# Encoder trunk, two layers on one core: the B-C products moved into a projection unit, and a re-divided entry

## The chip, the cores and the metric

The kernel runs on one NeuronCore of a Trainium2 chip. The metric is the device time of one execution in microseconds. A core has five engines with queues of their own: TensorE (PE; its weight loads are listed apart as PEld), VectorE (DVE), ScalarE (ACT), GpSimd (POOL) and SyncE (SP), which here only issues transfers. They meet at semaphores alone.

## The reference: what is computed

Two sequences of 256 tokens (512 tokens, width 1024) are layer-normalised and go through two layers:

```
proj = h @ w_in                       # q, k, v, z, x/B/C, dt
attn_out = window_attention(rope(q), rope(k), v, sink)
xbc = silu(depthwise_conv(xbc, w, b));  xs, bm, cm = split(xbc)
y = bidir_ssd(xs, dt_raw, dt_bias, a_log, bm, cm) + d * xs
ssd_out = rms_norm(y * silu(z), g)
h = layer_norm(alpha * h + concat(attn_out, ssd_out) @ w_out)
gate, val = split(h @ w_up);  gate = depthwise_conv(gate, w3, b3)
h = layer_norm(alpha * h + (silu(gate) * val) @ w_down)
```

In `bidir_ssd` each 128-token block needs the product of its C rows with the B rows (`einsum("bcqgn,bcsgn->bcgqs", cc, bc)`), in two groups. These are the B-C products of this change.

## The kernel before

**Units.** Every weight matrix is cut into units of 128x1024 (512 KB): 27 per layer for the input projection (unit 0 is dt, 1 k, 2 v, 3 to 6 q, 7 to 10 the B and C channels, 11 to 18 x, 19 to 26 z), 12 for the output projection, 44 up, 22 down. Five `raw`, `whi` and `wlo` slots form a ring. SP loads a unit into `raw`; `split` on ACT writes its high part `whi`. The low part `wlo` = raw - whi comes from DVE, or, for the units in `BY_DMA`, in two steps: ACT writes -whi, and a transfer issued by POOL adds the weights to it. A product is three fp32r matmuls (`by_columns`, `three`: high by high, high by low, low by high), 24 of 512 columns per unit of the projection.

**The order of the mixer.** `mixer_schedule()` writes one list, `SCHED`; each engine walks the whole list and does what concerns it. Step n has ("G", n), the unit's 24 matmuls, and around it the work of earlier units. The names that matter:

- AS, AM, AX, AD, AN, PT, AV (attention, eight items i = n - 8): scores on PE (L1255); mask, maximum and negation on DVE (L1622 to L1627); exponentials on ACT (L808); denominator and reciprocal on DVE (L1635); scaling of `sc` on POOL (L580); 32x32 transpose into `p_t` on DVE (L1648); values on PE in the middle of units 12, 14, 16 and 17 (`AV_AT`, L896), their low part `alo` on DVE (L1638).
- E, F, F1, F2, F3, SILU, SIL2 (the convolution): centre tap on ACT (L720), four taps on DVE (L1476), tanh on ACT (L755), the last product on DVE (L1483, into `bc` or `xsc`), counted by `silu_done`.
- T: transposes of an x channel block on PE (L1181), which wait for `silu_done` of its block. XS: product of `xsc` by a column on POOL (L588).
- CB: the B-C products, two fp32 matmuls of 256 columns for each block i = 0 to 3 (L1189), copied to `cb` by ACT (L781).
- MV: four `heads` tiles on POOL (L599). SB, SF: decay matmuls on PE (L1215, L1226). SC: their caps on DVE (L1579).

Small products (CB, T, VT, DTT, SD, AA, AO and the values' first claim) share banks 6 and 7 by turns: `wait_aux_free` lets a use begin when the one two before it has been read. The use two before CB(0) is the first value product, free once `alo` has been written (`al_done`). PE's queue is in order, so a product that waits holds the whole next unit.

**Entry.** PE runs 18 small matmuls (`keep_warm`, L905), then transposes the first two normalised token tiles (L1081), then 8 more, then `entry_units` begins units 0 to 2 (L917) on the first sequence. DVE takes moments and normalises all four token tiles; ACT makes the high part of unit 1 (`split(1)`) and then the activations' high part (`highs`, L648, L657); POOL makes the low part of the first sequence's activations (`lows(0)`, L550).

## Time and profile before

| | |
|---|---|
| median of 3 runs | 1298.28 us (1296.52 to 1298.59) |
| profiled execution | 1298.11 us |
| its span, first to last instruction | 1296.3 us (1.8 us lie around it) |
| mean granted TensorE clock | 0.998 |
| PE, PEld | 1280.9 us (99%), 1059.5 us (82%) |
| DVE, ACT, POOL | 801.7 us (62%), 609.2 us (47%), 131.0 us (10%) |
| chain that ended last | PE 92%, DVE 6%, ACT 1%, issue 1% |

Busy time is the time in which an instruction of the engine was under way. PE's matmuls overlap (one of 512 columns is listed with 390 ns, the next starts 0.23 us after it), so 99% busy hides short waits; those are read from start times. The shares of DVE, ACT and POOL are means over stages with very different loads.

### The profile page before, as it was taken

To read this page: it belongs to the slowest core of one execution; us is meant where nothing else is said; L and a number is where in the kernel's file an instruction comes from. 1 tells how busy PE (TensorE), PEld (TensorE's weight loads), DVE (VectorE), ACT (ScalarE), POOL (GpSimd) and SP (SyncE) were. 2 spreads that over 40 slices of the span, in tenths; PEclk is the share of its full clock that TensorE was granted. 3 is DMA by queue.
4 is the path that set the end of the run, shared out by engine and by line. 5 is a ranking of instruction groups with operands and counts; after the bars stand their busy time and mean duration, and the time that the engine had idled before them with its cause. 6 is when DMAs were issued, how large, how long until landed. Compare 5 with 4: busy or idle time off the path is not lost.

```text
span 1296.3 us, 17993 instructions
## 1 busy us (share of the span) xinstructions
PE 1280.9 (99%) x7456; PEld 1059.5 (82%) x7456; DVE 801.7 (62%) x1071; ACT 609.2 (47%) x913; POOL 131.0 (10%) x125
## 2 busy tenths in 40 slices
PE   9999999999999999999999999999999999999997
PEld 8877778889888888888898777788888888888886
DVE  7888898866444444342378998979654444443425
ACT  5766766436333333311276776653553333332112
POOL 2034511001000000000020354000100000000000
PEclk9999999999999999999999999999999999999999
DMA  5465565423333333323134656563133323223222
GB/s 200 158 147 115 132 146 138 172 77 103 98 98 98 98 98 98 130 98 97 54 127 150 151 114 150 129 179 130 66 114 98 98 98 96 96 93 129 96 95 111
DMA packets 43872, 151.36 MB, mean 117 GB/s; under 512 B 4912, under 2 KB 9424, under 8 KB 42640
## 3 DMA queue, kind: packets, MB, share of 16 engines
q1 hardware_dynamic: 38160, 130.01, 30.2%
q0 software_dynamic: 5632, 20.21, 9.1%
q8 instruction: 59, 0.97, 0.3%
q14 instruction: 21, 0.17, 0.0%
HBM read 141.81 MB, written 6.29 MB: 114 GB/s over the span
## 4 chain that ended last, share of the span: by engine, by line
PE 92%; DVE 6%; ACT 1%; issue 1%; DMA 0%; POOL 0%; SPq 0%; DVEq 0%
PE ps L870 17%; PE ps L871 17%; PE ps L872 17%; PE ps L1028 9%; PE ps L1029 9%; PE ps L1030 9%; PE ps L917 5%; PE ps L1242 2%; DVE cv L1476 2%; PE ps L896 1%; PE ps L1020 1%; DVE ast L1624 1%; PE ps L1189 1%; PE ps L1255 1%; PE ps L1226 1%
## 5 line engine op out<-in xcount | busy, mean ns | idle before, releaser
L870 PE MATMUL ps<-hhi,whi 128*128 128x512 f32 x1040 | 411.2, 395 | 0.9 <-DVE cv L1476 0.7
L871 PE MATMUL ps<-hlo,whi 128*128 128x512 f32 x1040 | 405.5, 390 | 0.0
L872 PE MATMUL ps<-hhi,wlo 128*128 128x512 f32 x1040 | 405.2, 390 | 0.0
L619 ACT ACTIVATE whi<-raw 128x1024 fp32r<-128x1024 f32 x208 | 219.4, 1057 | 214.6 <-DMA raw<-in_units 214.6
L1313 DVE TENSOR_TENSOR wlo<-raw,whi 128x1024 fp32r<-128x1024 f32 x170 | 207.8, 1224 | 149.4 <-ACT whi L619 149.4
L870 PEld LDWEIGHTS ps<-hhi,whi 128*128 128x128 f32 x1040 | 195.4, 188 | 49.3 <-issue 6.7
L872 PEld LDWEIGHTS ps<-hhi,wlo 128*128 128x128 f32 x1040 | 195.5, 188 | 41.3
L871 PEld LDWEIGHTS ps<-hlo,whi 128*128 128x128 f32 x1040 | 195.6, 188 | 39.4
L1028 PE MATMUL ps<-whi,uhi 128*128 128x512 f32 x352 | 137.1, 390 | 0.0
L1030 PE MATMUL ps<-wlo,uhi 128*128 128x512 f32 x352 | 137.0, 389 | 0.0
L1029 PE MATMUL ps<-whi,ulo 128*128 128x512 f32 x352 | 136.9, 389 | 0.0
L1689 DVE SCALAR_TENSOR_TENSOR gcv<-ps,pf,gcv 128x510 f32<-128x510 f32 x44 | 32.9, 749 | 157.3 <-ACT gcv L840 157.3
L840 ACT ACTIVATE gcv<-ps,pf 128x512 f32<-128x512 f32 x44 | 34.3, 780 | 169.0 <-PE ps L872 162.2
L1699 DVE TENSOR_TENSOR guf<-gsg,ps 128x512 f32<-128x512 f32 x44 | 30.2, 687 | 79.0 <-PE ps L872 78.4
L1476 DVE SCALAR_TENSOR_TENSOR cv<-ps,pm,cv 128x508 f32<-128x508 f32 (+1 forms) x96 | 71.4, 744 | 11.2 <-ACT cv L720 4.9
L1028 PEld LDWEIGHTS ps<-whi,uhi 128*128 128x128 f32 x352 | 66.1, 188 | 13.7
L1030 PEld LDWEIGHTS ps<-wlo,uhi 128*128 128x128 f32 x352 | 66.1, 188 | 13.7
L1029 PEld LDWEIGHTS ps<-whi,ulo 128*128 128x128 f32 x352 | 66.1, 188 | 13.6
L1028 PE MATMUL ps<-whi,ahi 128*128 128x512 f32 x192 | 75.8, 395 | 0.2
L1029 PE MATMUL ps<-whi,alo 128*128 128x512 f32 x192 | 74.8, 389 | 0.0
L1030 PE MATMUL ps<-wlo,ahi 128*128 128x512 f32 x192 | 74.7, 389 | 0.0
L550 POOL TENSOR_TENSOR hlo<-hfm,hhi 128x512 fp32r<-128x512 f32 x16 | 21.9, 1375 | 513.0 <-ACT hhi L657 512.7
(182 smaller groups left out, 1548.7 us busy)
## 6 DMA issues: line engine op xcount, KB each, us to landing
raw<-in_units SPq DMA_DIRECT2D x208, 512.0 KB, 3.5
wlo<-in_units POOLq DMA_DIRECT2D x38, 512.0 KB, 5.5
gb<-in_gb SPq DMA_DIRECT2D x5, 1024.0 KB, 5.5
h_kept<-hb SPq DMA_DIRECT2D x2, 2048.0 KB, 8.9
ha<-h_kept SPq DMA_DIRECT2D x2, 2048.0 KB, 9.6
hb<-in_x SPq DMA_DIRECT2D x4, 512.0 KB, 5.8
v_rep<-v_tm SPq DMA_DIRECT2D x32, 64.0 KB, 2.1
out_y<-hb SPq DMA_DIRECT2D x8, 256.0 KB, 2.0
```

Of the source, the lines that this page charges most:

```text
L619: A(whi[:, m % RING, :], raw[:, m % RING, :], ACT.Copy).then_inc(unit_hi, 1)
L840: A(gcv[:], ps[:, bank, :], ACT.Identity, scale=pf[:, k * 3 + w0 + 1:k * 3 + w0 + 2], bias=pf[:, k + v0:k + v0 + 1]).then_inc(glu_center, 1)
L870: mm(out, whi[:, slot, cols], xhi, start=start, stop=False)
L871: mm(out, whi[:, slot, cols], xlo, start=False, stop=False)
L872: return mm(out, wlo[:, slot, cols], xhi, start=False, stop=stop)
L917: last = mm(out, w, x, start=c == 0 and kind == "hi hi", stop=stop, skip_group_check=True)
L1028: mm(ps[:, bank, :], xhi[:, rows], whi[:, slot, cols], start=start, stop=False)
L1029: mm(ps[:, bank, :], xlo[:, rows], whi[:, slot, cols], start=False, stop=False)
L1030: return mm(ps[:, bank, :], xhi[:, rows], wlo[:, slot, cols], start=False, stop=stop)
L1313: V.tensor_tensor(wlo[:, m % RING, :], raw[:, m % RING, :], f(whi[:, m % RING, :]), ALU.subtract).then_inc(unit_split, 1)
L1476: V.scalar_tensor_tensor(out=dst[:, :, lo:hi], in0=src[:, :, lo + s:hi + s], scalar=pmc("conv_w", 5 * j + tap, 5 * j + tap + 1), in1=dst[: ...
L1689: V.scalar_tensor_tensor(out=dst[:, :, 1:SEQ], in0=src[:, :, 0:SEQ - 1], scalar=pf[:, k * 3 + w0:k * 3 + w0 + 1], in1=dst[:, :, 1:SEQ], op ...
```

## The change

It has four parts. (a) The B-C products of blocks 0 and 2 are issued by PE in the middle of units 13 and 15 (`CB_AT`, `mixed`), where they stood ahead of units 13 and 15; ACT copies them after its exponentials and not before. (b) Unit 11 joins `BY_DMA`: DVE's subtraction for it goes, ACT writes one more negated copy, POOL issues one more transfer. (c) On DVE the transpose PT goes ahead of the product SIL2 of the same step, and at n = 17 the caps SC(0) go ahead of SIL2; on POOL the `heads` tiles are made one step earlier. (d) At the entry ACT normalises the first token tile in two halves (`entry_act`), after DVE has written its shift (`entry_shift`); POOL makes the high part of unit 1 (`entry_high`); the second warm-up has 4 matmuls, not 8.

```diff
-BY_DMA = range(12, 31)
+BY_DMA = range(11, 31)
+CB_AT = {13: 0, 15: 2}
@@ mixer_schedule
-        if n in (13, 15):
+        if n in CB_AT:
             steps += [("CB", n - 12)]
-        if n in (12, 14):
-            steps += [("CB", n - 12)]
+        if n + 1 in CB_AT:
+            steps += [("CB", CB_AT[n + 1])]
         steps += [("SH" if n >= U_CONV else "S", n + AHEAD)]
...
         if 1 <= i < 8:
-            steps += [("SIL2", n - 1 - U_CONV)]
+            steps += [("PT", i - 1), ("SIL2", n - 1 - U_CONV)]
...
-            steps += [("PT", i - 1)]
+        if n == 15:
+            steps += [("MV", 0), ("MV", 1)]
...
             steps += [("SILU", n - U_CONV)]
+            if n == 17:
+                steps += [("SB", 0), ("SC", 0)]
...
-            if n == 17:
+            if n == 16:
                 steps += [("MV", 2), ("MV", 3)]
@@ POOL
+            def entry_high():
+                pool.wait_ge(raw_loaded[1], 16)
+                nc.gpsimd.tensor_copy(whi[:, 1, :], raw[:, 1, :]).then_inc(entry_hi, 1)
...
                 if L == 0:
+                    entry_high()
                     lows(0)
@@ ACT
+            act.wait_ge(entry_shift, 1)
+            for half in range(2):
+                x = hb[:, 0, half * 512:(half + 1) * 512]
+                A(x, x, ACT.Identity, scale=st[:, 0, 3:4], bias=st[:, 0, 0:1]).then_inc(entry_act, 1)
             split(0)
-            split(1)
             highs(0, 0)
@@ PE
+            def mixed(L, i):
+                pe.wait_ge(silu_done, L * N_CONV + 4)
+                wait_aux_free(pe, L, ("CB", i))
+                for g in range(2):
+                    last = mm(...)
+                last.then_inc(aux_full, 1)
...
-            keep_warm(8, 7)
+            keep_warm(4, 7)
...
-                        between = functools.partial(values, L, AV_AT[i]) if i in AV_AT else None
+                        between = None
+                        if i in AV_AT:
+                            between = functools.partial(values, L, AV_AT[i])
+                        elif i in CB_AT:
+                            between = functools.partial(mixed, L, CB_AT[i])
@@ DVE
-            normed_first(0)
+            rstd(0, 0)
+            dve.wait_ge(ln_rstd, 1)
+            V.tensor_scalar(st[:, 0, 0:1], st[:, 0, 1:2], st[:, 0, 3:4], -1.0, ALU.mult, ALU.mult).then_inc(entry_shift, 1)
             normed_first(1)
```

PE's queue between unit 12 and unit 13 of layer 0, before. `ps<-qk` are the scores AS(4), `ps<-bc` the B-C products of block 0, then comes unit 13; in brackets the semaphores that a row waits for.

```order
L872 MATMUL ps<-hhi,wlo 128x512
L1255 MATMUL ps<-qk 128x256 [waits as_exp]
L1255 MATMUL ps<-qk 128x256 x3
L1189 MATMUL ps<-bc 128x256 [waits al_done,silu_done]
L1189 MATMUL ps<-bc 128x256
L870 MATMUL ps<-hhi,whi 128x512 [waits low_added3,conv_taps]
L871 MATMUL ps<-hlo,whi 128x512
```

The same queue of the changed kernel, in the middle of unit 13:

```order
L882 MATMUL ps<-hhi,wlo 128x512
L917 MATMUL ps<-bc 128x256 [waits al_done,silu_done]
L917 MATMUL ps<-bc 128x256
L880 MATMUL ps<-hhi,whi 128x512
L881 MATMUL ps<-hlo,whi 128x512
```

The two products and their wait for `al_done` have moved behind the first 12 matmuls of unit 13; after the scores, unit 13 now begins at once.

DVE's queue at the end of step 12, before: reciprocal of item 4, the last tap, the product SIL2(4) into `xsc`, the transpose PT(3) into `p_t`, then the mask of item 5.

```order
L1635 RECIPROCAL ast<-ast 128x4 [waits dve_link]
L1476 SCALAR_TENSOR_TENSOR cv<-ps,pm,cv 128x2x254 [waits conv_taps,conv_center]
L1483 SCALAR_TENSOR_TENSOR xsc<-xsc,cv 128x512 [waits conv_tanh]
L1648 STREAM_TRANSPOSE p_t_73<-sc_70 128x4x8x32 [waits as_norm]
L1622 SCALAR_TENSOR_TENSOR ps<-cn,ps 128x4x128 [waits as_full]
```

And of the changed kernel:

```order
L1657 RECIPROCAL ast<-ast 128x4 [waits dve_link]
L1498 SCALAR_TENSOR_TENSOR cv<-ps,pm,cv 128x2x254 [waits conv_taps,conv_center]
L1670 STREAM_TRANSPOSE p_t_73<-sc_70 128x4x8x32 [waits as_norm]
L1505 SCALAR_TENSOR_TENSOR xsc<-xsc,cv 128x512 [waits conv_tanh]
L1644 SCALAR_TENSOR_TENSOR ps<-cn,ps 128x4x128 [waits as_full]
```

The product now stands behind the transpose; nothing else of the step has moved.

POOL's queue at the entry, before: the parameters' transfers, an instruction without a tile that the compiler puts ahead of the first `tensor_tensor` (printed ISA), the four low parts, and what follows them.

```order
L561 DMA pm<-in_pm 128x160 [waits x_loaded1]
L562 DMA pf<-in_pf 128x120
L550 ISA
L550 TENSOR_TENSOR hlo<-hfm,hhi 128x2x256 [waits ln_hi] x4
L566 MEMSET ln_dt 128x32x8 [waits ln_normed]
```

And of the changed kernel:

```order
L567 DMA pm<-in_pm 128x160 [waits x_loaded1]
L568 DMA pf<-in_pf 128x120
L559 CAST whi<-raw 128x1024 [waits raw_loaded1]
L551 ISA
L551 TENSOR_TENSOR hlo<-hfm,hhi 128x2x256 [waits ln_hi] x4
```

The copy and its wait for the weights' transfer stand ahead of both the ISA row and the four low parts.

## Rows read from the trace of the kernel before

**Rows 1.** Waits of PE, whole span (total us, times, longest):

```profile
PE ps L1226 <- DVE e_fwd L1579: 1.5, 2, 0.9
```

**Rows 2.** Timeline, PE, layer 0 (start us, us, instruction, idle before):

```profile
97.01 1.14 PE L1255 MATMUL ps<-qk 64*128 64x256 f32 x8
99.87 1.82 PE L1189 MATMUL ps<-bc 128*128 128x256 f32 x4 [1.73 <-DVE alo L1638]
...
108.01 1.14 PE L1255 MATMUL ps<-qk 64*128 64x256 f32 x8
```

**Rows 3.** Timeline, PE, the same place in layer 1:

```profile
737.36 1.13 PE L1255 MATMUL ps<-qk 64*128 64x256 f32 x8
740.18 1.10 PE L1189 MATMUL ps<-bc 128*128 128x256 f32 x4 [1.70 <-DVE alo L1638]
746.67 1.14 PE L1255 MATMUL ps<-qk 64*128 64x256 f32 x8
...
748.70 0.60 PE L1181 MATMUL ps<-cn,xsc 128*128 128x128 f32 x4
```

**Rows 4.** Table by stretch, layer 0 (us; PE, PEld, DVE, ACT, POOL busy; clock):

```profile
101.10:104.00 2.90, 2.90 (x9) 2.31 (x8) 2.58 (x7) 2.27 (x10) 0.00 (x0) 0.58 0.83 153
```

**Rows 5.** Timeline, DVE, layer 0, attention items 0 and 1:

```profile
68.36 0.70 DVE L1622 SCALAR_TENSOR_TENSOR ps<-cn,ps 128x512 f32<-128x512 f32 x1 [1.00 <-PE ps L1255]
...
70.83 1.22 DVE L1313 TENSOR_TENSOR wlo<-raw,whi 128x1024 fp32r<-128x1024 f32 x1
...
75.26 0.69 DVE L1622 SCALAR_TENSOR_TENSOR ps<-cn,ps 128x512 f32<-128x512 f32 x1
```

**Rows 6.** Timeline, PE, scores of items 0 and 1:

```profile
67.18 1.13 PE L1255 MATMUL ps<-qk 64*128 64x256 f32 x8
73.90 1.13 PE L1255 MATMUL ps<-qk 64*128 64x256 f32 x8
```

**Rows 7.** POOL, line 580 (ns min/median/max, first and last start):

```profile
L580 POOL TENSOR_TENSOR sc<-sc,ast x32: 1030/1038/1487, 74.8 to 772.4; 128x512 f32<-128x512 f32 x32
```

**Rows 8.** DVE, line 1483, the same columns:

```profile
L1483 DVE SCALAR_TENSOR_TENSOR bc<-bc,cv x8: 692/1110/1111, 66.7 to 737.2; 128x512 f32<-128x512 f32 x8
```

**Rows 9.** Timeline, layer 0, end of step 12, DVE and POOL:

```profile
105.41 1.11 DVE L1483 SCALAR_TENSOR_TENSOR xsc<-xsc,cv 128x512 f32<-128x512 f32 x1
106.44 1.23 DVE L1648 STREAM_TRANSPOSE p_t<-sc 128x1024 f32<-128x1024 f32 x1
109.19 0.70 DVE L1622 SCALAR_TENSOR_TENSOR ps<-cn,ps 128x512 f32<-128x512 f32 x1 [1.52 <-PE ps L1255]
...
104.94 2.48 POOL L580 TENSOR_TENSOR sc<-sc,ast 128x512 f32<-128x512 f32 x2 [5.22 <-DVE ast L1635]
```

**Rows 10.** Timeline, PE, from a unit's end into a group of small products:

```profile
125.76 0.39 PE L871 MATMUL ps<-hlo,whi 128*128 128x512 f32 x1
125.99 0.39 PE L872 MATMUL ps<-hhi,wlo 128*128 128x512 f32 x1
126.31 1.14 PE L1255 MATMUL ps<-qk 64*128 64x256 f32 x8
```

**Rows 11.** Timeline, DVE, layer 0, end of step 17:

```profile
149.98 1.46 DVE L1483 SCALAR_TENSOR_TENSOR xsc<-xsc,cv 128x512 f32<-128x512 f32 x1 [0.70 <-ACT xsc L755]
```

**Rows 12.** Timeline of the entry, ACT, DVE, POOL and PE:

```profile
9.02 1.06 ACT L619 ACTIVATE whi<-raw 128x1024 fp32r<-128x1024 f32 x1 [0.94 <-DMA raw<-in_units]
...
9.70 1.00 DVE L1399 TENSOR_SCALAR hfm<-ps,cn 128x256 f32<-128x256 f32 x2 [0.43 <-PE ps L1081]
10.62 0.41 DVE L1310 TENSOR_TENSOR whi<-raw,whi 128x256 fp32r<-128x256 f32 x1
...
14.83 1.10 DVE L1373 TENSOR_SCALAR hb<-hb,st 128x1024 f32<-128x1024 f32 x1
...
11.59 5.47 POOL L550 TENSOR_TENSOR hlo<-hfm,hhi 128x512 fp32r<-128x512 f32 x4 [4.36 <-ACT hhi L657]
...
15.99 1.09 PE L1020 MATMUL ps<-cn,hb 128*128 128x128 f32 x8
```

More of the change, by code:

```diff
@@ L161, in mixer_schedule @@
                 steps += [("SL", n - 1 + AHEAD)]
-        if 15 <= n < 17:
-            steps += [("MV", n - 15)]
-        if n == 17:
-            steps += [("SB", 0), ("SC", 0)]
-        elif a >= 0:
+        if a >= 0:
             if a >= 1:
@@ L357, in trunk @@
         h_low, h_lows, entry_low = sem("h_low"), sem("h_lows"), sem("entry_low")
+        entry_shift, entry_act, entry_hi = sem("entry_shift"), sem("entry_act"), sem("entry_hi")
         entry_cols, entry_tp = sem("entry_cols"), sem("entry_tp")
@@ L616, in split @@
                     if m % UNITS == U_DT:
-                        A(dt_part(whi, m, 0), dt_raw(m), ACT.Copy).then_inc(unit_hi, 1)
+                        A(dt_part(whi, m, 0), dt_raw(m), ACT.Copy).then_inc(unit_hi, 1 if m else 2)
                     else:
@@ L900, in values @@
                 last.then_inc(aux_full, 1)
+            def mixed(L, i):
+                pe.wait_ge(silu_done, L * N_CONV + 4)
+                wait_aux_free(pe, L, ("CB", i))
+                for g in range(2):
+                    last = mm(ps[:, aux_bank(("CB", i)), g * SEQ:(g + 1) * SEQ], bc[:, g, i * BLK:(i + 1) * BLK],
+                              bc[:, 2 + g, i // 2 * SEQ:(i // 2 + 1) * SEQ], start=True, stop=True)
+                last.then_inc(aux_full, 1)
             def keep_warm(n, bank):
@@ L926, in entry_units @@
                     part(0, 0, 0, 0, "hi hi", (2 * j, 2 * j + 1))
-                pe.wait_ge(unit_hi, 2)
+                pe.wait_ge(entry_hi, 1)
                 part(0, 0, 1, 0, "hi hi", range(4))
@@ L1076, in _ @@
                 for t in range(2):
-                    pe.wait_ge(ln_normed, 2 if t and half else 1)
-                    if t and not half:
+                    if t == 0:
+                        pe.wait_ge(entry_act, half + 1)
+                    elif half:
+                        pe.wait_ge(ln_normed, 2)
+                    else:
                         pe.wait_ge(entry_cols, 1)
@@ L1183, in _ @@
                         last.then_inc(aux_full, 1)
-                    elif what == "CB":
-                        pe.wait_ge(silu_done, L * N_CONV + 4)
-                        wait_aux_free(pe, L, (what, i))
-                        b = i // 2
-                        for g in range(2):
-                            last = mm(ps[:, aux_bank((what, i)), g * SEQ:(g + 1) * SEQ], bc[:, g, i * BLK:(i + 1) * BLK],
-                                      bc[:, 2 + g, b * SEQ:(b + 1) * SEQ], start=True, stop=True)
-                        last.then_inc(aux_full, 1)
+                    elif what == "CB" and i not in CB_AT.values():
+                        mixed(L, i)
                     elif what == "VT":
@@ L1307, in split @@
                 if m < DEPTH * UNITS and not by_dma(m):
-                    dve.wait_ge(unit_hi, m + 1)
+                    dve.wait_ge(*((entry_hi, 1) if m == 1 else (unit_hi, m + 1)))
                     if m % UNITS == U_DT:
@@ L1370, in normed_first @@
                         V.tensor_scalar(x, x, st[:, t, 1:2], st[:, t, 3:4], ALU.subtract, ALU.mult).then_inc(
-                            ln_normed if half else entry_cols, 1)
+                            ln_normed if half else entry_cols, 1 + half)
                 else:
```

## The prediction

> **What bounds the kernel now.** I read the table of busy times first: PE is busy for 99% of the span and ends the chain for 92% of it. A matmul of 512 columns starts 0.23 us after the one before it, less than its listed length, so a busy share can't show a short wait. The second view is therefore the list of PE's waits, and the third the timeline around each. Two waits of the mixer stand out, each once per layer. The decay matmuls after unit 18 wait 1.5 us in all (0.6 and 0.9) for DVE's caps [rows 1]. The B-C products of block 0 wait 1.73 us in layer 0 and 1.70 us in layer 1 for the values' low part on DVE [rows 2, 3].
>
> The wait in layer 0 has a second price. From the scores of item 4 to those of item 5 PE takes 11.00 us in layer 0 and 9.31 us in layer 1, though the queue is the same [rows 2, 3]: 1.69 us more. The table by stretch shows why: right behind the wait the granted clock is 0.58, so most of that stretch ran at 1.2 GHz and not at 2.4 [rows 4]. Before it PE had stood still. Layer 1 had the same wait and kept its clock, so such a wait may cost 1.7 us more or nothing.
>
> Last I looked at what the products wait for. From item 1 on (75.26, no idle ahead of it) DVE works without a pause; the first idle time ahead of a mask comes again at item 5, 1.52 us, released by PE [rows 5, 9]. So between items 1 and 5 DVE sets the pace and PE waits, and from there on PE does. A gain in the stretch needs an earlier DVE, and a PE that has other work than the waiting row.
>
> **The change part by part.**
>
> *Unit 11's subtraction leaves DVE.* It took 1.22 us, in the step of item 0 [rows 5]. But the mask of item 1, eight rows further on in that queue, needs the scores of item 1. Those start at 73.90; for item 0 DVE began 1.18 us after the scores did (67.18, 68.36), so item 1 can begin at 75.08 and began at 75.26 [rows 5, 6]. All but 0.18 us of the 1.22 goes into idle time. The other side is hidden: ACT's extra copy (about 1.06 us, as the high part in rows 12) lies in step 7, where ACT waits for PE and DVE; the extra transfer is issued four units ahead of its use; nothing but the scaling of `sc`, two units away, is queued behind it on POOL.
>
> *The transpose ahead of the product.* In these steps the product takes 1.11 us where it takes 0.69 undisturbed [rows 8], and POOL's scaling takes 1.04 us in one half of its instructions and 1.49 in the other [rows 7]. That is the picture of turns: the product waits 0.42 us for the scaling under way, then the second scaling waits for the product. The Trainium skill (SBUF — State Buffer, Who interferes with whom) says the same as a rule: a DVE instruction with two SBUF inputs and a GpSimd instruction that reads SBUF exclude each other for a whole instruction, and one with a single input does not meet GpSimd. With the transpose in front, POOL's pair (104.94 plus 2 x 1.04) ends at 107.02. The transpose holds DVE from 105.41 to about 106.56 (its length less the 0.08 by which DVE's rows overlap), so the product may start only at 107.02 and ends at 107.71 [rows 7 to 9]. With the transpose behind it, it ended at 106.52. The pair of instructions costs DVE the same 2.2 us as before; what changes is that `silu_done` comes 1.2 us later in each such step. I take this value. The other end is that turns don't matter and the product takes 0.69: then each step saves 0.42 us of DVE.
>
> *The B-C products in mid-unit.* Take layer 1, which has no change of clock. The scores of item 4 start at 737.36, 0.18 earlier now, and take 2.82 - 1.70 = 1.12 us; unit 13 follows at once. From the products to the next scores it was 6.49 us, and scores and products together are 748.70 - 746.67 = 2.03, so the products are 0.91 and the unit 5.58 [rows 3]. A group of small products in mid-unit costs an entry more: 0.32 us from the last large matmul to the group in place of 0.23 [rows 10], and about as much behind it: 0.2 with both. Next scores: 737.18 + 1.12 + 5.58 + 0.91 + 0.2 = 744.99, in place of 746.67. Products of block 1 follow, and PE is ready for the transposes T(4) at 747.02.
>
> What is late next is the operand of T(4), the product of step 12. By the paragraph above it ends at 107.71 - 0.18 = 107.53 in layer 0, which is 747.88 in layer 1's times (the scores of item 4 lie 640.35 us apart) [rows 2, 3, 9]. T(4) started at 748.70 and will start at about 747.9: the new wait of 0.9 us eats half of what the move won, and the gain is 0.8 us a layer. In bounds: 1.7 if the product isn't late at all, 0 if `silu_done` is 0.8 us later still. Behind T(4) stands unit 14. From there PE sets the pace again (the 1.52 us of idle DVE), so the gain stays; the second moved group (block 2) had no wait to lose and costs 0.2. That makes 0.6 a layer, 1.2 in all. ACT, which now meets its copy of block 0 behind its exponentials, is waited for by T(4) only, and is done first.
>
> *Caps ahead of the product in step 17.* The product stood 1.46 us ahead of the caps [rows 11]; both waits for them (0.6, 0.9) are shorter than that, and the caps' own input is ready. 1.5 us are gained; the least is 0.7, if the caps were held half a step by something unseen.
>
> *The clock.* The wait of 1.7 us goes; one of 0.9 a layer appears. I take it that the clock stays up: 1.7 us.
>
> *Entry.* DVE's first tile goes to ACT, but the transposes of the two tiles then follow each other on PE, and DVE's first `hfm` comes about 0.1 us earlier (9.6). POOL's copy can start when the weights have landed, at 9.0, as ACT's did [rows 12]. It has no row. Below: a scaling of 512 elements with two inputs, which reads as many elements, 1.03 us [rows 7]. Above: POOL's other conversion to fp32r in this stage, 5.47 / 4 = 1.37 us for 512 columns, 2.7 for 1024 [rows 12]. I take 2.7, since it is the same stage and the same neighbours. It then ends at 11.7. The low part of the dt unit on DVE (10.62, two SBUF inputs) comes up at 10.5 and by the turns of above waits until 11.7. Everything behind it on DVE is 1.1 us late, down to the normalised third tile, which ended at 15.93 and for which PE's transposes at 15.99 had no slack: 17.1, a loss of 1.1 us [rows 12]. ACT, freed of 1.06 us of copying, would have given POOL's low parts (from 11.59) up to 0.4 us; the copy's end at 11.7 takes that away. Bounds: a gain of 0.3 with a copy of 1.03 us, a loss of 1.1. The four warm-up matmuls less come off ahead of a wait and gain nothing.
>
> **Sum**, against the profiled execution: 1298.11 - 1.7 (clock) - 1.2 (products) - 1.5 (caps) + 1.1 (entry) = 1294.8. It stood 0.2 us under the median of its runs, so 1295.0.
>
> **The rivals.**
>
> *The clock falls again.* PE now stands still for 0.9 us ahead of each T(4), and for over a microsecond behind the shorter warm-up. One fall costs 1.7 us: 1296.7. For it speaks that one wait of two brought a fall; against it, that the new ones are half as long.
>
> *Turns don't matter.* The product takes 0.69 in steps 9 to 12 and the entry's copy holds nobody: up to 1.1 us more a layer, 1292.8, and 1291.7 with the entry at no loss. For it: nobody has seen transpose and scaling side by side at length. Against it: the two lengths of the scaling.
>
> *The wait only moves.* If the product of step 12 comes another 0.8 us late, the products' move gives nothing and costs 0.4: 1296.6.
>
> *The entry turns on POOL, slower side.* The compiler puts an instruction without a tile ahead of the first low part. Before, it lay in POOL's idle 4.36 us, which ended with ACT's high part and not with it [rows 12]: it takes between 0 and 4.3 us, and nothing waited. Now it stands behind the copy, on the path. With 4.3 us the low parts start at 16.0 in place of 11.6, 4.4 late instead of 1.1, PE waits over 4 us for them, and the clock falls: 1295.0 + 3.3 + 1.7 = 1300.0. Slower than before begins at about 2.5 us of it, with the fall. Against it: the idle time ahead of the first low part ended with ACT's row and not later. If the instruction loads code, the Trainium skill (GPSIMD Engine Reference, Instruction dispatch) puts a first call after a load at about 6 us; by that figure it would have ended at 13.2, and the trace has the first low part at 11.59, so here the trace disagrees and most likely nothing is loaded.
>
> **How the numbers follow.** What a measurement of this kernel can tell from no change is about 0.2%, 2.6 us: faster is under 1295.7, slower over 1300.9. Chances: the forecast 0.40; turns don't matter, in part or whole, 0.18; the clock falls once or twice 0.22; the wait moves 0.08; POOL's instruction 0.12, half of it over 1300.9 with a second fall. Faster 0.57, same 0.36, slower 0.07. The likeliest gives 1295.0. The range reaches down into the second case (1292.3) and up past the first and third, with a part of the fourth (1298.6).
>
> **What would show it.** Right: no idle row of PE ahead of `ps<-bc` in either layer; an idle of 0.5 to 1.2 us ahead of the transposes of `xsc` in step 13, released by DVE's product; the product 1.1 us long, the scaling always 1.04; no wait for `e_fwd`; a granted clock of 1 throughout; POOL's copy of 2 to 3 us and DVE's `whi` row behind its end. Wrong: PE's first low-part matmul later than 15 us; a stretch at 0.5 anywhere; a product of 0.7 in steps 9 to 12.

## The result and the profile after

The changed kernel took **1305.39 us** (median of 4 executions, 1305.1 to 1308.1) against 1298.42 us for the kernel before on the same chip: ratio 1.006, 95% interval 1.0046 to 1.0075. It is slower, by an interval clear of 1; the forecast was 1295.0 and a gain. Its profiled execution has a span of 1303.7 us, 7.4 more than before, and a mean granted clock of 0.994 where it was 0.998. Measured again later in 11 executions it took 1303.97 us (1298.0 to 1305.9), ratio 1.0035 (1.0023 to 1.0046).

The list of PE's waits of the changed kernel (total us, times, longest):

```profile
PE ps L906 <- issue: 4.0, 2, 2.3
PE ps L1207 <- DVE alo L1660: 2.7, 1, 2.7
...
PE ps L1207 <- DVE xsc L1505: 0.9, 2, 0.5
```

The waits that the change was to remove are gone: there is none for `e_fwd` [rows 1], none ahead of the B-C products [rows 2, 3]. Two others are in their place. PE waits twice for "issue", which means that the profile shows nothing it waited for, and it does so in L906, the matmuls of the values AV. And the transposes (L1207) wait once, 2.7 us, for the values' low part `alo`. The small wait for `xsc` is the one that was forecast ahead of T(4).

The timeline of PE, changed kernel (start us, us, instruction, idle before). L906 are the values, L1275 the scores, L1207 the transposes T: in layer 0 the rows at 106.87, 139.06, 150.11, 158.32 and 164.70 are T(4), T(7), T(8), T(9) and T(10). Up to 165 us it is layer 0, from 743 layer 1:

```profile
96.57 1.13 PE L1275 MATMUL ps<-qk 64*128 64x256 f32 x8
104.21 1.13 PE L1275 MATMUL ps<-qk 64*128 64x256 f32 x8
106.87 0.66 PE L1207 MATMUL ps<-cn,xsc 128*128 128x128 f32 x4 [0.47 <-DVE xsc L1505]
110.21 2.04 PE L906 MATMUL ps<-p_t,v_rep 32*64 32x128 f32 x122
114.56 0.70 PE L906 MATMUL ps<-p_t,v_rep 32*64 32x128 f32 x6 [2.31 <-issue]
120.61 1.34 PE L1275 MATMUL ps<-qk 64*128 64x256 f32 x8
139.06 0.60 PE L1207 MATMUL ps<-cn,xsc 128*128 128x128 f32 x4
150.11 0.63 PE L1207 MATMUL ps<-cn,xsc 128*128 128x128 f32 x4 [2.72 <-DVE alo L1660]
158.32 0.60 PE L1207 MATMUL ps<-cn,xsc 128*128 128x128 f32 x4
164.70 0.60 PE L1207 MATMUL ps<-cn,xsc 128*128 128x128 f32 x4
743.03 1.13 PE L1275 MATMUL ps<-qk 64*128 64x256 f32 x8
753.32 0.66 PE L1207 MATMUL ps<-cn,xsc 128*128 128x128 f32 x4 [0.46 <-DVE xsc L1505]
774.99 1.83 PE L906 MATMUL ps<-p_t,v_rep 32*64 32x128 f32 x107
778.54 0.66 PE L906 MATMUL ps<-p_t,v_rep 32*64 32x128 f32 x21 [1.72 <-issue]
786.87 2.09 PE L906 MATMUL ps<-p_t,v_rep 32*64 32x128 f32 x128
```

The rows of the kernel before that answer to them and stand in no group above (L896 are its values, L1181 its transposes, L1226 the decay matmuls):

```profile
110.04 0.60 PE L1181 MATMUL ps<-cn,xsc 128*128 128x128 f32 x4
113.34 2.09 PE L896 MATMUL ps<-p_t,v_rep 32*64 32x128 f32 x128
118.31 1.14 PE L1255 MATMUL ps<-qk 64*128 64x256 f32 x8
136.52 0.60 PE L1181 MATMUL ps<-cn,xsc 128*128 128x128 f32 x4
144.97 0.60 PE L1181 MATMUL ps<-cn,xsc 128*128 128x128 f32 x4
151.51 0.60 PE L1181 MATMUL ps<-cn,xsc 128*128 128x128 f32 x4
158.74 0.60 PE L1181 MATMUL ps<-cn,xsc 128*128 128x128 f32 x4
770.30 2.09 PE L896 MATMUL ps<-p_t,v_rep 32*64 32x128 f32 x128
778.48 2.09 PE L896 MATMUL ps<-p_t,v_rep 32*64 32x128 f32 x128
791.38 0.70 PE L1226 MATMUL ps<-heads,off_w 128*128 128x512 f32 x2 [0.88 <-DVE e_fwd L1579]
```

From such pairs of rows nearly the whole difference adds up. A step is the distance between two starts in one kernel, against the same distance in the other:

| stretch | before | after | difference |
|---|---|---|---|
| up to the scores of item 4 | 97.01 | 96.57 | -0.44 |
| these scores to T(4), layer 0 | 13.03 | 10.30 | -2.73 |
| the same in layer 1 | 11.34 | 10.29 | -1.05 |
| AV(1) to the scores of item 6, layer 0 | 4.97 | 10.40 | **+5.43** |
| T(7) to T(8), layer 0 | 8.45 | 11.05 | **+2.60** |
| T(8) to T(9), layer 0 | 6.54 | 8.21 | **+1.67** |
| T(9) to T(10), layer 0 (the caps) | 7.23 | 6.38 | -0.85 |
| AV(2) to AV(3), layer 1 | 8.18 | 11.88 | **+3.70** |
| the caps, layer 1 (the idle 0.88 us) | | | -0.88 |

The sum is +7.45; the spans differ by 7.4. The stretches that the table leaves out differ by up to 0.3 us each and cancel. So the gains came, 5.95 us of them, and 13.4 us of new losses ate them. The table by stretch says that part of each loss is the clock. Its rows give the stretch and its length, the busy time of PE, PEld, DVE, ACT and POOL, then the granted clock, the DMA share and GB/s; they stand after the first wait for "issue", after the one for `alo`, and after the second for "issue":

```profile
114.50:121.00 6.50, 6.44 (x20) 4.49 (x22) 0.80 (x2) 0.88 (x2) 1.85 (x2) 0.50 0.49 83
152.00:155.30 3.30, 3.30 (x9) 2.60 (x8) 3.20 (x4) 1.90 (x3) 0.00 (x0) 0.51 0.99 159
780.10:783.30 3.20, 3.20 (x9) 2.52 (x8) 2.19 (x3) 0.00 (x0) 3.20 (x2) 0.51 0.02 5
```

At 0.50 the granted clock is at its lower level of 1.2 GHz, and half of such a stretch is lost: 3.3, 1.7 and 1.6 us. PE had stood still for 2.31, 2.72 and 1.72 us ahead of them.

**The wait for `alo`.** The timeline of DVE and POOL, changed kernel (L1505 is the product SIL2, L606 the `heads` tiles, L1660 `alo`):

```profile
139.60 1.85 DVE L1505 SCALAR_TENSOR_TENSOR xsc<-xsc,cv 128x512 f32<-128x512 f32 x1
145.37 3.99 DVE L1505 SCALAR_TENSOR_TENSOR xsc<-xsc,cv 128x512 f32<-128x512 f32 x1 [0.70 <-ACT xsc L765]
149.29 0.68 DVE L1660 TENSOR_TENSOR alo<-ps,ahi 128x512 fp32r<-128x512 f32 x1
...
139.00 4.21 POOL L606 TENSOR_TENSOR heads<-cum_a,cn 128x1024 fp32r<-128x1024 f32 x2
144.75 4.06 POOL L606 TENSOR_TENSOR heads<-cum_a,cn 128x1024 fp32r<-128x1024 f32 x2
```

A product of 0.69 us undisturbed is listed with 3.99. Less those 0.69 it could begin at 148.67, and POOL's two tiles end at 148.81. One product earlier it is 1.85, and there the engines took turns: by the rows of single tiles the first ends at 140.90, the product, less its 0.69, begins at about 140.8, and the second, from 140.86, is listed with 2.35 us for 2.03, so it waited for the product. The changed schedule issues two `heads` tiles just ahead of each of these products; only the second one was held through both. Before, it was one tile at a time, and the pair that followed later held the product at 149.98 us for 0.8 us only [rows 11]. T(8) needs a bank that `alo` frees, and so waits with it. (The expectations below call this group T(9); counted from T(4), one after each unit, it is T(8).)

**The wait for "issue".** It begins in the middle of 128 matmuls that wait for nothing. Weight loads and matmuls together, a values product is 256 instructions in 2.1 us. The table of DMA queues has a kind "instruction", q8: 59 packets and 0.97 MB over the span, 16 KB each; PE and PEld together are 14,896 instructions in the trace, 252 for each packet. So these packets look like PE's own code, and a values product uses one up in 2.1 us. The DMA view of the changed kernel for 107 to 112.2 us, and the packet counts for 112.2 to 114 (packets, MB, share of 16 engines):

```profile
DMA  3300000000000000000995446946799997979999
...
q0 software_dynamic: 120, 0.49, 54.3%
...
q0 software_dynamic: 24, 0.03, 10.4%
q8 instruction: 1, 0.02, 3.3%
```

From 109.4 us, when POOL's transfer for `wlo` (q0) begins to move data, there is no instruction packet until 112.36, when that transfer is almost over, and PE goes on 2.2 us later. In layer 1 the packet comes at 776.25, again with the last part of a transfer of q0, and PE goes on 2.3 us later. The Trainium skill (Runtime: NRT & Kernel Launch, Instruction fetch mechanics) states the blocks as 16 KiB or 256 instructions, fetched through a DMA queue of the sequencer's own, at a cost that is "mostly hidden". The size agrees with the 252; "hidden" doesn't here.

### The profile page after: what moved, and what is told of

Its sections match the earlier page's. It is cut to its first block, busy times and chain, and to the rows that moved or that the text cites. A ratio compares the mean times of both kernels' runs of the same rounds, so it can differ in the third digit from the quotient of the medians.

```text
span 1303.7 us, 17981 instructions
## 1 busy us (share of the span) xinstructions
PE 1285.8 (99%) x7448; PEld 1062.0 (81%) x7448; DVE 799.4 (61%) x1069; ACT 611.7 (47%) x916; POOL 128.6 (10%) x128
## 4 chain that ended last, share of the span: by engine, by line
PE 91%; DVE 7%; issue 1%; ACT 0%; POOL 0%; DMA 0%; DVEq 0%
PE ps L880 17%; PE ps L882 17%; PE ps L881 17%; PE ps L1047 9%; PE ps L1048 9%; PE ps L1049 9%; PE ps L936 5%; PE ps L1262 2%; DVE cv L1498 2%; PE ps L1039 1%; DVE p_t L1670 1%; DVE ast L1646 1%; PE ps L906 1%; PE ps L1275 1%; DVE xsc L1505 1%
```

## The experiments

Two theories. **H**: the `heads` tiles moved a step earlier hold DVE's product, with it `alo` and T(8): 2.7 us and a half clock, that is, a stretch behind it at 1.2 GHz. **F**: PE's code blocks come late, because a transfer stands ahead of them and because a block boundary falls near the end of a values product. Rivals: the transpose in front of the product does it; the waits hang on timing or on the position of the code alone. Beside each the kernel before ran on the same chip, and ratios are to it: kernels 1 to 4 (kernel n is that of experiment n) on one chip, 5 to 8 on a second, 9 to 12 on a third, 13 to 15 on the first again; the kernel before had medians of 1299.0, 1298.9, 1300.0 and 1298.8 us there. Between kernels of different groups a difference of two times can be a microsecond off; the one by the ratios is then given too.

**1. The heads tiles in their old places.** (`heads_late`)

```diff
-        if n == 15:
-            steps += [("MV", 0), ("MV", 1)]
-            if n == 16:
+            if n == 17:
                 steps += [("MV", 2), ("MV", 3)]
+        if 15 <= n < 17:
+            steps += [("MV", n - 15)]
```

> The changed kernel with only POOL's four heads tiles back in their old places (two of them one step later, two at n = 17). Theory H: the two pairs of heads tiles (4.21 and 4.06 us) are what stretches DVE's product to 1.85 and 3.99 us in layer 0; the low part of the last values comes 2.72 us late, PE stands still ahead of T(9), and half the clock behind it costs 1.7 us more. Then this kernel has no such wait, no half clock near 152 us, a product of 0.7 us there, and takes 1305.4 - 2.7 - 1.7 = about 1301.0 us. Rival: the low part is late because of the transpose in front of the product, or because the values themselves come late; then the 2.7 us stay and the time stays within 1 us of 1305.4.

Measured: 1296.67 us (1294.4 to 1302.1, 12 executions), ratio 0.9991 (0.9977 to 1.0006). In its profile the product ahead of the last `alo` takes 0.69 us again and no transpose waits for `alo`; the product before that one, with a single tile beside it, still takes 1.84. The profiled execution, at 1302.08, was the slowest of the twelve, and still 3.4 us under the changed kernel's (8.7 by median, and 7.3 against the changed kernel's later 1303.97). It had both waits for "issue", longer than before (2.58 and 2.28 us), which accounts for 0.8 of the 4.4 expected. H holds. The new thing is the spread: 7.7 us between executions of one program. The fastest, 1294.4, has a mean clock of 0.999, the slowest 0.994, which suggests that the waits come in some executions and not in others; only the slowest has a profile.

**2. The product ahead of the transpose again.** (`product_first`)

```diff
-            steps += [("PT", i - 1), ("SIL2", n - 1 - U_CONV)]
+            steps += [("SIL2", n - 1 - U_CONV)]
             ...
+            steps += [("PT", i - 1)]
```

> The changed kernel with DVE's product SIL2 back ahead of the transpose PT in steps 9 to 15; everything else stays. Theory F: PE stands still within the values (2.31 us in layer 0, 1.72 in layer 1, no wait on a semaphore) because a 16 KB block of its instructions comes late, behind a transfer of wlo; the block is asked for late since T(4) waits 0.47 us for the product and POOL's transfer is issued only after the product. With the product 1.2 us earlier, T(4) waits no more and the transfer is issued 1.2 us earlier: no stall in either layer, no half clock behind it (6.8 and 3.4 us at half speed are 3.4 and 1.7 us lost), so about 1305.4 - 2.3 - 3.4 - 1.7 - 1.7 = 1296.3 us. Rival 1: the transpose's place has nothing to do with it; stalls stay, time within 1 us of 1305.4. Rival 2: the product now meets the scaling by turns and takes 1.11 us again, T(4) waits as before; then the time falls by less than 1 us.

Measured: 1303.59 us (1302.7 to 1304.2), ratio 1.0036 (1.0024 to 1.0048). The waits within the values stayed (3.08 and 1.46 us), and so did the one for `alo` in layer 0 (2.49). My account of why the block is late by way of T(4) and the product is wrong. Rival 1 holds in the main: the time is 1.8 us under the first measurement of the changed kernel and 0.4 under the later one. T(4) did stop waiting for the product.

**3. Code shifted by 84 instructions.** (`shifted_code`)

```diff
+            for _ in range(21):
+                mm(ps[0:32, 7, 0:32], avg[0:32, 0:32], avg[0:32, 0:32], start=True, stop=True)
             keep_warm(18, 7)
```

> The changed kernel with 21 tiny matmuls (32x32) more ahead of the first warm-up, where PE waits for the input anyway: all later PE instructions stand 84 instructions further on against the 16 KB blocks in which they are fetched, and nothing else changes. Theory F: a values product is some 256 PE instructions in 2.1 us, a whole block; it stalls only where a block boundary falls near its end, as after 122 of 128 matmuls in layer 0 and 107 of 128 in layer 1. The shift puts these boundaries at about 80 and 65, so both stalls vanish or turn up in other values at other counts, always at a boundary; time 1296 to 1305 us. Rival: the stall has nothing to do with where the code stands (a semaphore, a queue of weight loads, memory); then it stays at the same two places with the same lengths, and the time stays within 0.5 us of 1305.4.

Measured: 1301.82 us (1299.5 to 1304.1), ratio 1.0024 (1.0014 to 1.0033). The tiny matmuls took 2.45 us, more than PE had idle there, and made the entry 1.2 us later; the rest of the kernel is some 3 to 5 us shorter. The wait of 2.71 us for `alo` is in layer 1 here and not in layer 0. The timeline of PE, values of layer 0:

```profile
129.76 2.06 PE L906 MATMUL ps<-p_t,v_rep 32*64 32x128 f32 x124
133.87 0.43 PE L906 MATMUL ps<-p_t,v_rep 32*64 32x128 f32 x4 [2.05 <-issue]
...
141.95 1.63 PE L906 MATMUL ps<-p_t,v_rep 32*64 32x128 f32 x94
145.31 0.86 PE L906 MATMUL ps<-p_t,v_rep 32*64 32x128 f32 x34 [1.73 <-issue]
```

AV(1) and the second layer have no such wait any more; it turned up in AV(2) after 124 matmuls and in AV(3) after 94. Between these two stops lie 4 matmuls, half a unit (12), the 4 transposes, another 12 and 94: 126, each with a weight load, 252 instructions. PE stops where one block ends and the next begins. I had hoped that the two boundaries would move out of harm's way; they did, and two others moved in.

**4. Both undone.** (`heads_late_product_first`)

```diff
-        if n == 15:
-            steps += [("MV", 0), ("MV", 1)]
+        if 15 <= n < 17:
+            steps += [("MV", n - 15)]
...
-            steps += [("PT", i - 1), ("SIL2", n - 1 - U_CONV)]
+            steps += [("SIL2", n - 1 - U_CONV)]
...
+            steps += [("PT", i - 1)]
```

> Both undone: heads tiles in their old places and the product ahead of the transpose; the B-C products in mid-unit, the caps ahead of the product at n = 17, unit 11 by transfer and the entry stay. If theories H and F both hold the gains add: 1305.4 - 4.4 - 9.1 = 1291.9 us, faster than the kernel before by 0.5%. If only H holds, 1301.0; if only F, 1296.3; if neither, 1305.

Measured: 1297.56 us (1294.8 to 1300.0), ratio 0.9986 (0.9974 to 0.9999), with 4.7 us in two waits for "issue" in its profile and no long wait for `alo`. Of the two cures only that of H works.

**5. The changed kernel once more.** (`after_again`)

> The changed kernel unchanged, beside the next three on the same chip. Its four times so far were 1305.1 to 1308.1 us, while the kernel with the heads tiles late, whose profiled execution was only 3.4 us shorter, spread from 1294.4 to 1302.1 over 12 executions. If the waits within the values come and go from execution to execution, this kernel spreads as well, from about 1299 (no such wait, but the one ahead of T(9) and its half clock) to 1308; if they are fixed, all executions lie within 1305 to 1308.

Measured: 1303.97 us (1298.0 to 1305.9, 11 executions). It spreads as well: its fastest execution has a clock of 0.999, and most lie from 1303 to 1306.

**6. Heads late, and 48 PE instructions fewer at the entry.** (`heads_late_block_shift`)

```diff
-            keep_warm(18, 7)
+            for _ in range(6):
+                mm(ps[:, 7, 0:3 * P].rearrange("p (a b) -> p a b", a=3), avg[:],
+                   avg[:].unsqueeze(1).broadcast_to((P, 3, P)), start=True, stop=True)
```

> The kernel with the heads tiles late, and the first warm-up of PE made of 6 matmuls of 384 columns where it had 18 of 128: the same columns in the same time, but 48 PE instructions fewer, so that all that follows stands 48 instructions (24 pairs of a weight load and a matmul) earlier against the 16 KB blocks. Theory F: boundaries now stand at about matmul 18 of AV(1), 62 of AV(2), 32 of AV(3) in layer 0 and at 3 of AV(2) and 101 of AV(3) in layer 1; at most the last can stall, so the time falls from 1296.7 to about 1294.5, and the spread of the executions narrows. Rival: where the code stands doesn't matter beside the timing of the transfers; waits of 1.5 to 2.5 us stay in AV(1) and AV(2), median within 0.7 us of 1296.7.

Measured: **1293.59 us** (1293.0 to 1294.3), ratio 0.996 (0.9948 to 0.9972), 3.1 us under kernel 1 (4.0 by the ratios, whose intervals don't meet) and a spread of 1.3 us in place of 7.7. Its timeline of PE in layer 1:

```profile
768.81 0.39 PE L880 MATMUL ps<-hhi,whi 128*128 128x512 f32 x1 [0.89 <-issue]
774.18 1.76 PE L906 MATMUL ps<-p_t,v_rep 32*64 32x128 f32 x101
776.44 0.68 PE L906 MATMUL ps<-p_t,v_rep 32*64 32x128 f32 x27 [0.50 <-issue]
```

AV(3) of layer 1 stops after 101 matmuls, the number that was forecast from the count of instructions. In layer 0 the packet comes as late as in the changed kernel, at 112.87 us, but no boundary stands in the values there, and PE doesn't stop. The columns of the warm-up are the same, and PE's transposes of the third token tile begin at 15.89 us, in kernel 1 at 16.05, so the edit acts by where the code is cut into blocks; nothing else in the profile accounts for 3 us.

**7. Units 17 and 19 by DVE.** (`heads_late_two_by_dve`)

```diff
-BY_DMA = range(11, 31)
+BY_DMA = sorted(set(range(11, 31)) - {17, 19})
```

> The kernel with the heads tiles late, with the low parts of units 17 and 19 made by DVE's subtraction again (1.22 us each) in place of POOL's transfer: the transfer that is issued at 107.9 us in layer 0 and its counterpart at AV(2) in layer 1 fall away, the code of PE stays where it is. Theory F: PE's instruction block, which came only when that transfer was over (112.5 us, after 122 of 128 matmuls), now comes as soon as it is asked for; no wait in AV(1) of layer 0 nor in AV(2) of layer 1, no half clock behind them; 1294.5 us, and steady. DVE's 1.22 us lie in its idle 1.5 us of steps 13 to 16, at a cost of at most 0.5. Rival: the block is late on its own account, because 256 instructions are used up in 2.1 us; then both waits stay as they are and the time stays within 0.7 of 1296.7 or rises.

Measured: 1299.32 us (1295.0 to 1303.1), ratio 1.0004 (0.9992 to 1.0016). The expectation named the wrong units: what POOL issues in step 13 is the transfer of unit 16, and it was still there. In the profile the wait in layer 0 was absent all the same, and the one in layer 1 was 2.95 us, behind a transfer. As a test of the transfer it is inconclusive, and was repeated with the right units (11). But its trace says more. PE reached AV(1) at 110.42 us, as in kernel 1 (110.40); here the instruction packet came at 108.0, ahead of the first packets of the transfer (109.6), and PE ran through all 128 matmuls, while in kernel 1 it came at 112.7, and PE stopped for 2.58 us after 122. So with the same boundary and the same transfer PE stops or doesn't, by which of the two comes first. That fits the spread of the executions.

**8. The products' move alone** (`products_alone`), on the kernel before.

```diff
+CB_AT = {13: 0, 15: 2}
...
-        if n in (12, 14):
-            steps += [("CB", n - 12)]
+        if n + 1 in CB_AT:
+            steps += [("CB", CB_AT[n + 1])]
...
```

> The kernel before with the B-C products in the middle of units 13 and 15 alone; all other parts of the change left out. By the prediction's step: 1.7 us less with the clock kept, and 0.6 to 1.7 a layer, with the 0.4 us turn of the product as before: 1298.4 - 1.7 - 2.4 = 1294.3. By theory F the move brings AV(1) 3 us ahead against POOL's transfer, so the waits within the values should already be there: then 1294.3 plus 2 to 8, about 1298 and spread over several us.

Measured: 1297.5 us (1293.7 to 1299.2, 12 executions), ratio 0.9981 (0.997 to 0.9992). Its profile has AV(1) stopped for 3.23 us after 113 matmuls and not after 122: it has the long second warm-up, 8 pairs of instructions more, ahead of them. Four executions lie at 1293.7, all with a clock of 0.999, and most others around 1298. So the waits within the values need neither the swap, nor unit 11, nor the heads: bringing PE 3 us forward is enough.

**9. The kernel before, both warm-ups wide** (`before_block_shift`) (as in 6, and 4 matmuls of 256 columns for the second 8: 64 instructions fewer, which puts its code in the frame of kernel 6).

```diff
-            keep_warm(18, 7)
+            for _ in range(6):
+                mm(ps[:, 7, 0:3 * P]..., avg[:], avg[:].unsqueeze(1).broadcast_to((P, 3, P)), start=True, stop=True)
-            keep_warm(8, 7)
+            for _ in range(4):
+                mm(ps[:, 7, 0:2 * P]..., avg[:], avg[:].unsqueeze(1).broadcast_to((P, 2, P)), start=True, stop=True)
```

> The kernel before with its two warm-ups made of fewer and wider matmuls (6 of 384 columns for 18 of 128, 4 of 256 for 8 of 128): the same columns, 64 PE instructions fewer, so that its values stand against the 16 KB blocks exactly as in the kernel of 1293.6 us. Theory F: the profile of before has only one such wait (0.25 us at AV(3)), so the shift gains little: its executions of 1300 us and more come together at 1296.5 to 1298.5, median about 1298, and the 5 us between it and 1293.6 are the edits'. Rival: the gain of 1293.6 is the shift's alone, and this kernel comes to about 1294 to 1295 as well.

Measured: 1297.69 us (1296.9 to 1298.8), ratio 0.999 (0.9981 to 0.9999). The frame, which is where the block boundaries fall, gives the kernel before 1.3 us by the ratio (2.3 by the medians) and a narrower spread; the edits give the other 4. Its profile has the same wait of 1.72 us ahead of the B-C products, and this time no half clock behind it (granted clock 1.00 from 101.1 to 104 us, where it was 0.58 [rows 4]).

**10. The changed kernel in the good frame** (`after_block_shift`), heads tiles early.

```diff
-            keep_warm(18, 7)
+            for _ in range(6):
+                mm(ps[:, 7, 0:3 * P]..., avg[:], avg[:].unsqueeze(1).broadcast_to((P, 3, P)), start=True, stop=True)
```

> The changed kernel with the first warm-up of 6 wide matmuls, heads tiles early as in the change. This prices the heads move alone, without the waits within the values: theory H says 2.7 us of wait ahead of T(9) in layer 0 and 1.7 us behind it at half clock, 1293.6 + 4.4 = 1298.0 us, and steady. Rival: the heads early cost more (they also hold the products and transfers of layer 1), 1300 or over; or less, if the wait comes only where the values were late before it: then T(9) waits under 1 us and the time is under 1295.

Measured: 1299.33 us (1297.8 to 1301.0), ratio 0.9998 (0.999 to 1.0007). Against kernel 6 the heads' move alone costs 5.7 us (4.9 by the ratios). In its profile T(8) waits 2.72 us in layer 0, as in the changed kernel, and the second layer's transposes 1.06 us as well, which I had not counted.

**11. Units 16 and 18 by DVE** (`heads_late_units_16_18_by_dve`), heads late, code where the change put it.

```diff
-BY_DMA = range(11, 31)
+BY_DMA = sorted(set(range(11, 31)) - {16, 18})
```

> The kernel with the heads tiles late, code where it was, with the low parts of units 16 and 18 by DVE in place of POOL's transfer. In the run with 17 and 19 the transfers that lie ahead of AV(1) in layer 0 (issued at 107.9 us, unit 16) and of AV(2) in layer 1 (unit 18) were still there, and so was the wait in layer 1, 2.9 us, with the block landing when the transfer was over. If the block waits behind that transfer, both waits go now and the executions lie near 1294.5, but for what DVE's extra 1.22 us cost (up to 3 us, as 17 and 19 seem to have cost). If the block is late on its own account, waits of 1 to 3 us stay in AV(1) of layer 0 (after 122 matmuls) and in AV(2) of layer 1 (after 107) though no transfer lies ahead of them.

Measured: 1294.2 us (1293.85 to 1294.55), ratio 0.9965 (0.9952 to 0.9979), 2.5 us under kernel 1 (3.4 by the ratios) and steady. Its timeline at AV(1) of layer 0, and its DMA view for 107 to 112.2 us:

```profile
110.21 2.05 PE L906 MATMUL ps<-p_t,v_rep 32*64 32x128 f32 x122
...
112.58 0.44 PE L906 MATMUL ps<-p_t,v_rep 32*64 32x128 f32 x6 [0.32 <-issue]
...
DMA  4300000000000000000000600000000000000000
...
q8 instruction: 1, 0.02, 1.6%
```

The boundary is at the same matmul, 122. With no transfer ahead of it the instruction packet comes at about 109.9 (the 23rd of 40 slices), in the changed kernel at 112.36, and the wait is 0.32 us, not 2.31. Layer 1 has none. DVE's two subtractions more bring a wait for `alo` of 0.55 us in each layer. So in these profiles a long stop has two conditions: the boundary near the end of the values, and a transfer of POOL in front of the packet.

**12. Block shift and the product first.** (`block_shift_product_first`)

The edit is that of kernel 6 and:

```diff
-            steps += [("PT", i - 1), ("SIL2", n - 1 - U_CONV)]
+            steps += [("SIL2", n - 1 - U_CONV)]
```

> The kernel of 1293.6 us (heads tiles late, 48 PE instructions fewer) with the product ahead of the transpose again in steps 9 to 15. This prices the swap alone. By the prediction's step the swap makes the transposes T(4) wait 0.9 us a layer; its profile showed 0.4 us a layer, so the product first gives 1293.6 - 0.8 = 1292.8 us. Rival: with the product first DVE's turn with the scaling costs it 0.42 us in each of four steps, and the mask and the values come later: 1294 to 1296 us.

Measured: **1292.83 us** (1292.7 to 1293.9), ratio 0.9955 (0.9942 to 0.9969), the fastest of all. By this the swap costs 0.8 us (0.6 by the ratios); the executions of the two kernels overlap, so the size is uncertain.

**13. The products' move with the block shift** (`products_and_shift`), on the kernel before.

The edit is that of kernels 8 and 9 together:

```diff
+CB_AT = {13: 0, 15: 2}
-            keep_warm(18, 7)
+            for _ in range(6):
+                mm(ps[:, 7, 0:3 * P]..., avg[:], avg[:].unsqueeze(1).broadcast_to((P, 3, P)), start=True, stop=True)
...
```

> The kernel before with the B-C products in mid-unit alone and with both warm-ups wide (64 PE instructions fewer), so that no block boundary lies near the end of a values product. By the prediction's step with T(4) not late: 1.7 us a layer. Against before_block_shift, 1297.7 us: 1297.7 - 3.4 = 1294.3, or 1293.5 if a half clock now and then in the latter's executions goes as well. Rival: the products move gives under 1 us a layer, and caps, entry and unit 11 make up the rest of the 4.9 us to 1292.8: then this takes 1295.7 or more.

Measured: 1294.21 us (1293.8 to 1296.1), ratio 0.9966 (0.9953 to 0.9978): 3.5 us under kernel 9 (3.1 by the ratios), 1.6 to 1.7 a layer.

**14. The same and the caps ahead of the product.** (`products_caps_and_shift`)

```diff
             steps += [("SILU", n - U_CONV)]
+            if n == 17:
+                steps += [("SB", 0), ("SC", 0)]
...
-        if n == 17:
-            steps += [("SB", 0), ("SC", 0)]
...
```

> The same with SB(0) and SC(0) also ahead of the product at n = 17. The prediction's step: 1.5 us less. In the profile of before_block_shift, though, only one wait of 0.9 us for the caps was left, in layer 0, so by that 0.9 us less than products_and_shift. Rival: the product that now stands behind the caps comes 2.4 us later and its transposes wait; then no gain.

Measured: 1293.54 us (1293.0 to 1294.0), ratio 0.9958 (0.9945 to 0.997). The caps give 0.7 us, with executions of the two kernels that overlap a little (1293.8 to 1296.1 and 1293.0 to 1294.0).

**15. The same and units 16 and 18 by DVE.** (`products_caps_shift_16_18`)

```diff
-BY_DMA = range(12, 31)
+BY_DMA = sorted(set(range(12, 31)) - {16, 18})
```

> The same again with the low parts of units 16 and 18 by DVE in place of POOL's transfer. By theory F the small waits that were left in layer 1 of the shifted kernels (0.9 and 0.5 us behind AV(2) and in AV(3)) shrink, 0.5 to 1 us less. Rival: DVE's 2.4 us more a layer delay the masks and the low part of the values, and the time rises by up to 1 us, as the waits of 0.5 us ahead of the transposes in the run with 16 and 18 by DVE hint.

Measured: 1295.81 us (1295.7 to 1296.5), ratio 0.9976 (0.9966 to 0.9985): 2.3 us more. PE waits four times, 4.1 us in all, for `alo`. Here the rival holds, and by more than it said: the cure of kernel 11 has a price of its own on DVE.

## Why the prediction was wrong

Its terms were mostly right or too cautious; what failed is what it left out.

- **"One in layer 0 and one in layer 1": the products.** Right mechanism. From the scores of item 4 to those of item 5 it now takes 7.64 us in both layers, forecast 7.81. The second small group was charged 0.2 us and costs 0.04 (8.04 for 8.00 in kernels 10 and 9). T(4) waits 0.47 us, not 0.9. Sized at 1.2 us; the profile shows 1.05 in layer 1 with the swap, and kernel 13 shows 3.1 to 3.5 for both layers without it.
- **The swap and turns.** The product is listed from 105.86 us with 0.95, so it waits 0.26 us for the scaling under way. It ends 10.24 us after the scores of item 4; the forecast had 10.70, mostly because DVE and POOL come to this place 0.3 us earlier after those scores than they did. That the swap delays `silu_done` was right, and it costs some 0.8 us (kernels 6 and 12). Scaling always 1.03, as said. The mask of item 1 stands behind 0.87 us of idle DVE, so unit 11's subtraction lay in a gap, as said.
- **The caps, 1.5 us.** No wait for `e_fwd` is left, but alone they give about 0.7, the lower bound: of the two waits of [rows 1], one is missing in the later profile of kernel 9.
- **The clock, 1.7 us.** The half clock behind the products' wait went, but it was no fixed cost of the kernel before: in kernel 9 the same 1.72 us of wait has none. "I take it that the clock stays up" failed at three other places, behind waits of 1.7 us and more that the forecast didn't have.
- **The entry, a loss of 1.1 us.** Wrong sign. POOL's copy took 1.04 us, the lower bound, and not 2.7; DVE's first split went ahead at 10.62, and the instruction ahead of the low parts cost nothing. PE's transposes come 0.15 us earlier (15.84). Kernels 14 and 12, which differ by the entry and unit 11 alone, lie 0.7 us apart (0.4 by the ratios), in favour of the change.

The rows for the entry, changed kernel:

```profile
8.82 1.04 POOL L559 CAST whi<-raw 128x1024 fp32r<-128x1024 f32 x1 [1.64 <-DMA raw<-in_units]
11.44 5.47 POOL L551 TENSOR_TENSOR hlo<-hfm,hhi 128x512 fp32r<-128x512 f32 x4 [1.59 <-ACT hhi L664]
```

- **The step that failed first: the list of parts.** The `heads` tiles moved a step earlier, which the text on the change lists and the sum has no term for. The prediction had weighed POOL against DVE's product for the scaling and the entry's copy, by the very rule that holds here, and never asked which long POOL instructions the move puts beside a product with two SBUF inputs. It took this cost for nothing; it was 4.9 to 5.7 us (kernel 10 against 6). Nor is what the turn may cost bounded by one POOL instruction: two tiles, 4.06 us, held the product to their end, though one product earlier the same two let it in between them. The rule of the Trainium skill (SBUF — State Buffer, Who interferes with whom) has the loser wait a whole instruction; the trace shows one in the first case and two in a row in the second, and no run here shows what decides between them.
- **The second: PE's own code as a supply.** The sum has it at nothing too, and no rival considered that PE could wait for its instructions. The trace of before showed the sign: 256 instructions in 2.1 us, an instruction queue among the DMAs, and, in layer 0, a values product of 2.34 us in place of 2.09 at AV(3). Bringing PE 3 us forward against POOL's transfers, at the boundary as it stood, made it cost 9 us in the profiled execution.

Without these two the forecast's kernel exists: kernel 6, at 1293.6 us, 1.4 under the 1295.0 that was forecast. That it lies so near is in part luck, since errors of the terms offset each other: the products' move was worth 3.1 to 3.5 us and not 1.2, the clock's 1.7 us are no fixed gain, the caps gave 0.7 and not 1.5, the entry gained where a loss of 1.1 was charged, and the frame, with 1.3 us or more, stands in no term.

## What to carry to other kernels

When a move is priced, list every instruction that changes place, also those on an engine that is 10% busy: here two `heads` tiles of 2.03 us each, put beside a product of 0.69 us, held it for 3.3 us, and what waited for it the same. A stretch in which PE issues hundreds of tiny matmuls is also a stretch in which it needs code; look for big transfers just before it, and if PE stops "for issue" at the same matmul in every profile, shift the code against the blocks somewhere harmless and measure again. One shift may only move the stop to another product (kernel 3), another may end it (kernel 6). A kernel whose executions spread over several us with the mean clock falling may have a wait that is only sometimes there; two of its profiles are better compared before anything is explained.

## What the runs showed that I had not expected

- PE's code comes in packets of 16 KB (59 for 14,896 recorded instructions), and can be late: up to 3.2 us of wait (kernel 8). From the packet's start to the next matmul it took 2.2 to 2.6 us (112.36 to 114.56 in the changed kernel, 112.7 to 115.02 in kernel 1, 109.95 to 112.58 in kernel 11).
- The same program with 48 PE instructions fewer, and the same work, is 3.1 to 4.0 us faster and spreads over 1.3 us in place of 7.7.
- A DVE product with two SBUF inputs was held through two POOL instructions in a row, 3.99 us for 0.69; another, 6 us earlier, was let in between two.
- POOL converts 1024 fp32 columns to fp32r in 1.04 us, where its subtraction with an fp32r output takes 1.37 for 512.
- What stays open: what asks for a block, and when. In the kernel before a packet came at 109.6 us, among the packets of a weight transfer of SP (q1) and ahead of POOL's, whose data began to move at about 111; in the changed kernel, where PE was 3 us further on, it came at 112.36. That it was asked for earlier and stood behind POOL's transfer is inferred from the times alone.
